# An opening in another order: modulation pieces ahead of the input, six tiles from slots and banks of their own, and heads, gates and projections rearranged

## The chip, the cores and the metric

The kernel runs on one core of a Trainium2 chip. The metric is the device time of one execution in microseconds (us); of several runs the median is taken. A core has five engines with queues of their own, which work through their instructions in order: TensorE (PE, with PEld for its weight loads), VectorE (DVE), ScalarE (ACT), GpSimd (POOL) and SyncE (SP, which here only issues DMAs). They wait for each other through semaphores. PSUM, the memory that TensorE writes to, has eight banks of 128 partitions by 512 float32.

## What is computed

One layer of a decoder: a Mamba-2 mixer and a mixture of experts, both modulated by a vector c. `x` is 512 tokens by 1024 features, all in float32. The reference, cut to what matters here:

```python
c_act = jax.nn.silu(c)
mod = c_act @ ada_w + ada_b                      # 1024 -> 6 * 1024
sh1, sc1, g1, sh2, sc2, g2 = split(mod, 6)
hin = x * (1.0 + sc1) + sh1
z, xbc, dt = split(hin @ w_in, [2048, 2048 + 3072])        # 32 columns are dt
xbc = silu(causal_depthwise_conv(xbc, conv_w, conv_b))     # 4 taps
dt = softplus(dt + dt_bias); a = -exp(a_log)               # 32 heads in 4 groups
y = ssd_chunked_scan(xs, dt, a, bm, cm) + d_skip * xs      # decay, state, y
y = y * silu(z)
y = rms_norm(y, per group of 512) * norm_g
x = layer_norm(ALPHA * x + (1.0 + g1) * (y @ w_out), ln1_g, ln1_b)
hin = x * (1.0 + sc2) + sh2
eid, wts = route(hin, router_w, router_b)                  # 2 of 16 experts
x = layer_norm(ALPHA * x + (1.0 + g2) * moe_ffn(hin, eid, wts, ...), ln2_g, ln2_b)
```

## The kernel before

**Stages.** The program has three: the opening (to 98 us), four turns, one for each of the four head groups of eight heads (98 to 484 us, the fourth of them written out as the last turn), and the experts (from about 500 us to the end). All work is ordered by hand: each engine has its own block of code, and its instructions run in the order in which they stand there. SyncE's block is the order of nearly all loads.

**How a float32 product is made.** A weight unit is 128 by 1024 float32 (512 KB). ScalarE rounds it to the shorter type fp32r (`unit_high`, L712), GpSimd subtracts that from the original (`unit_low`, L566), and TensorE multiplies high by high, high by low and low by high. So one tile of a projection is 8 chunks x 3 = 24 products of 128x512 (L1576 to L1578). Raw units are staged in two slots of `stage`, the split ones in two slots of `wsplit`; s_uh, s_ul and s_unit count highs, lows and finished tiles, and SyncE may load a unit when the low half of the unit two before it is made.

**The opening.** SyncE loads c, the input `x` (four DMAs into `oacc`), then eight pieces of `ada_w` of 128x2048 float32 (1 MB; the last in two halves, 7a and 7b), then weight units. ScalarE's queue issues the small loads (ld_small) and w_dt, the 32 dt columns of w_in (ld_wdt). VectorE sums the pieces, each times a column of silu(c), into `accA` (L1009, L1014); row 0 of accA was first filled with ada_b through a DMA that waits for two memsets (L348), and before its first sum VectorE copies the transposed small rows out of PSUM (L1000 to L1004). TensorE transposes x, and from accA makes shift and scale as columns (modulation products, s_modp), which VectorE copies to `modc`. Then come `hin = x * (1 + scale) + shift` (L1031), its high half by ScalarE (L719), its low half by GpSimd or VectorE (L572, L1020), the products for dt (L1601 to L1603), and six x tiles of group 0: B, C and four of xs.
Each tile goes through `conv0` (ScalarE, last tap with bias, L741, reads the tile's bank), three more taps (VectorE, `xbc_tile`, L1048, read the same bank) and SiLU (ScalarE, L747). Two banks are used in turn, so tile i waits for the taps of tile i-2 (s_cv). Between the taps stand the dt steps on VectorE (L1239 to L1289): softplus of dt (with an exponential and a logarithm by ScalarE and a reciprocal, L1255), dt times a, a running sum (L1267), splitting of that into halves, four scalings by `gmask` into `acg`, a cast of `every8` (L1283), and the weights of the state. From these TensorE makes the products L1610 and transposes L1614 behind tile 5. GpSimd sets `oacc` to zero (L579) once x has been transposed, and sends it by two DMAs to the buffer in DRAM in which the experts' results are added (L582).

**A turn.** For each of the eight heads VectorE scales (`seg_head`, L1058), ScalarE takes exponentials (L755, L758), VectorE mixes (`mix_head`, L1067), GpSimd makes the decayed C (L589), and TensorE makes rows of decays (L1621) and, for two heads at once, y (`y_pair`, L1644 and L1646). Four state steps (`state_step`, L1080 to L1086) stand among the heads. `skip` and `gate` (L1143, L1150) follow for four pieces q of y, then squares (ScalarE) with their sums (GpSimd, L602), high halves of y (ScalarE) and low halves (VectorE, L1193), and TensorE's sums of squares (L1816). ScalarE's `zcopy` (L751) empties the banks of the z tiles. In between TensorE makes the next group's tiles and projects y with w_out.
In the last turn there is no next group. TensorE makes three pieces of the gate vector g1 (`mod_piece`, L1653) instead, two between y_pair(1) and y_pair(2) and one behind y_pair(3), then the sums of squares, and then the projection with w_out (`project`, L1676 to L1678), which waits for all four low halves. Thereafter a residual, layer norm and the routing lead to the experts.

## Time and profile before

| | |
|---|---|
| Runs of the kernel | 1084.26 us median of 3 (1082.76 to 1088.03) |
| Profiled execution | 1094.05 us, its span 1092.3 us |
| Granted TensorE clock, mean of the span | 0.979 of full speed |
| Busy share of the span | TensorE 94%, VectorE 83%, ScalarE 57%, GpSimd 42% |
| DMA | 285.17 MB, mean 261 GB/s |

The profile is of one execution. The span runs from the first instruction to the last. What each row says: in the timeline, a start and a length in us, the engine, the line of the kernel, the operation, what it writes and reads, and in brackets how long its engine had been idle, and which engine, buffer and line ended that. A clock of 1.00 in a stretch is the higher of TensorE's two levels (2.4 GHz), 0.50 the lower (1.2 GHz). Names of engines with a q behind (SPq) are the queue's own instructions, which issue DMAs.

### The profile page before, as it was taken

The numbers are of one execution on the slowest core, as the hardware profiler recorded it, in microseconds if no ns is written. First come the engines' busy times: TensorE is split into PE (matmuls) and PEld (weight loads), VectorE is DVE, ScalarE is ACT, GpSimd is POOL, SyncE is SP. The second block draws the span as 40 slices with busy tenths as digits, with TensorE's granted clock in tenths as the row PEclk, the third lists the DMA queues.
The fourth block names the chain that finished last, engine by engine and source line by source line (L and its number), as shares of the span: only waits on it lengthen the run. The fifth ranks groups of instructions, "written<-read, shape, count | busy, mean of one in ns | idle before, by whom it ended". The sixth has DMA issues, their size and how long they took to land.

```text
span 1092.3 us, 14992 instructions
## 1 busy us (share of the span) xinstructions
PE 1032.1 (94%) x4950; PEld 820.1 (75%) x4950; DVE 906.5 (83%) x964; ACT 617.2 (57%) x598; POOL 463.0 (42%) x298
## 2 busy tenths in 40 slices
PE   2697999999999997998999999999999999999997
PEld 2475788778778875874488888888888888888883
DVE  4897878787877877686498999998999999998986
ACT  0363463365256336350377777776777777776761
POOL 1343554465365445107043433244233433244467
PEclk9598999999999999999999999999999999999999
DMA  9337227324622735669389999999999999999992
GB/s 360 91 86 261 59 78 242 95 67 154 191 58 77 239 115 190 267 227 352 138 311 373 383 378 357 392 377 374 358 369 391 378 365 361 382 377 376 372 347 78
DMA packets 100565, 285.17 MB, mean 261 GB/s; under 512 B 9924, under 2 KB 51052, under 8 KB 83255
## 3 DMA queue, kind: packets, MB, share of 16 engines
q1 hardware_dynamic: 93890, 272.73, 68.5%
q0 software_dynamic: 5264, 11.86, 2.8%
q10 hardware_dynamic: 1382, 0.21, 0.1%
q8 instruction: 16, 0.26, 0.1%
q14 instruction: 13, 0.11, 0.0%
HBM read 276.60 MB, written 15.73 MB: 268 GB/s over the span
## 4 chain that ended last, share of the span: by engine, by line
PE 81%; DVE 10%; issue 3%; DMA 2%; ACT 2%; POOL 1%; ACTq 0%; DVEq 0%; SPq 0%; POOLq 0%
PE ps L1886 15%; PE ps L1888 15%; PE ps L1890 15%; PE ps L1576 5%; PE ps L1577 5%; PE ps L1578 5%; PE ps L1907 2%; PE ps L1836 2%; PE ps L1838 2%; PE ps L1837 2%; DVE ssd L1009 2%; PE ps L1879 1%; DMA both<-in_ssd_a_log 1%; PE ps L1870 1%; DVE ssd L1048 1%
## 5 line engine op out<-in xcount | busy, mean ns | idle before, releaser
L1312 DVE TENSOR_TENSOR moe_r<-moe,moe_r 128x2048 fp32r<-128x2048 f32 x180 | 412.7, 2311 | 58.2 <-ACT moe_r L891 58.2
L891 ACT ACTIVATE moe_r<-moe 128x2048 fp32r<-128x2048 f32 x180 | 344.8, 1928 | 124.1 <-PE ps L1890 119.1
L1886 PE MATMUL ps<-moe_r 128*128 128x512 f32 x720 | 211.2, 397 | 0.1
L1888 PE MATMUL ps<-moe_r 128*128 128x512 f32 x720 | 205.8, 390 | 0.0
L1890 PE MATMUL ps<-moe_r 128*128 128x512 f32 x720 | 205.5, 390 | 0.0
L566 POOL TENSOR_TENSOR ssd_r<-ssd,ssd_r 128x1024 fp32r<-128x1024 f32 x56 | 137.0, 2447 | 151.1 <-ACT ssd_r L712 147.2
L1890 PEld LDWEIGHTS ps<-moe_r 128*128 128x128 f32 x720 | 135.2, 188 | 29.1
L1888 PEld LDWEIGHTS ps<-moe_r 128*128 128x128 f32 x720 | 135.1, 188 | 29.1
L1886 PEld LDWEIGHTS ps<-moe_r 128*128 128x128 f32 x720 | 131.9, 188 | 26.6 <-DVE moe_r L1312 0.8
L1576 PE MATMUL ps<-ssd_r 128*128 128x512 f32 x320 | 128.6, 402 | 4.0 <-DVE ssd L1048 4.0
L640 POOL DMA_INDIRECT ydram<-moe,moe_i x14 | 31.1, 2225 | 224.7 <-DVE moe L1430 224.7
L1577 PE MATMUL ps<-ssd_r 128*128 128x512 f32 x320 | 125.8, 393 | 0.0
L1578 PE MATMUL ps<-ssd_r 128*128 128x512 f32 x320 | 125.6, 393 | 0.0
L630 POOL TENSOR_SCALAR moe_r<-both,moe_r 128x128 fp32r<-128x128 f32 x68 | 102.0, 1512 | 3.6 <-POOL moe_r L626 3.6
L712 ACT ACTIVATE ssd_r<-ssd 128x1024 fp32r<-128x1024 f32 x54 | 56.9, 1053 | 42.1 <-PE ps L1838 36.8
L1576 PEld LDWEIGHTS ps<-ssd_r 128*128 128x128 f32 x320 | 60.7, 190 | 19.4 <-DVE ssd L1048 4.4
L1577 PEld LDWEIGHTS ps<-ssd_r 128*128 128x128 f32 x320 | 60.8, 190 | 13.1 <-issue 1.0
L1578 PEld LDWEIGHTS ps<-ssd_r 128*128 128x128 f32 x320 | 60.8, 190 | 13.0
L1048 DVE SCALAR_TENSOR_TENSOR ssd<-ps,ssd 128x511 f32<-128x511 f32 (+2 forms) x72 | 56.6, 786 | 10.1 <-ACT ssd L741 8.3
L626 POOL CAST moe_r<-moe 128x20 fp32r (+1 forms) x17 | 16.5, 971 | 93.3 <-PE ps L1860 93.3
L589 POOL TENSOR_TENSOR ssd<-ssd 128x384 f32<-128x384 f32 x32 | 37.4, 1178 | 41.5 <-ACT ssd L758 41.5
L1058 DVE TENSOR_SCALAR ssd<-ps,ssd 128x128 f32<-128x128 f32 x128 | 43.7, 404 | 10.1 <-PE ps L1621 7.5
(302 smaller groups left out, 1474.7 us busy)
## 6 DMA issues: line engine op xcount, KB each, us to landing
moe<-in_moe_w_up SPq DMA_DIRECT2D x116, 1024.0 KB, 7.1
moe<-in_moe_w_down SPq DMA_DIRECT2D x64, 1024.0 KB, 8.0
ssd<-in_ssd_w_in SPq DMA_DIRECT2D x40, 512.0 KB, 4.0
ssd<-in_ada_w SPq DMA_DIRECT2D x30, 512.0 KB, 4.7
raw<-in_moe_w_up SPq DMA_DIRECT2D x12, 1024.0 KB, 7.7
ssd<-in_ssd_w_out SPq DMA_DIRECT2D x16, 512.0 KB, 4.7
ssd<-in_ada_w SPq DMA_DIRECT2D x4, 1024.0 KB, 16.4
ydram<-both POOLq DMA_DIRECT2D x2, 2048.0 KB, 13.0
```

The costliest lines, as they stand in the source:

```text
L566: pool.tensor_tensor(to[:, 1, :], stage[:, slot, :], to[:, 0, :].bitcast(F32), ALU.subtract).then_inc(s_ul, 1)
L630: op = pool.tensor_scalar(sel[:, t, :], iota, tabc[:, t, 4:5].bitcast(F32), None, ALU.is_equal)
L712: act.activation(wsplit[:, slot, 0, :], stage[:, slot, :], ACT.Identity).then_inc(s_uh, 1)
L891: act.activation(wr[:, part_slot(i), 0, :], ring[i % RING], ACT.Identity).then_inc(s_wh, 1)
L1048: op = dve.scalar_tensor_tensor(conv[:, i % 2, s:], ps[:, i % 2, 0:T - s], gtaps[:, k, i:i + 1], conv[:, i % 2, s:], ALU.mult, ALU.add)
L1312: dve.tensor_tensor(wr[:, part_slot(i), 1, :], ring[i % RING], wr[:, part_slot(i), 0, :].bitcast(F32), ALU.subtract).then_inc(s_wl, 1)
L1576: mm(to, wh[:, k, :], hin[:, 0, k, :], start=(k == 0), stop=False)
L1577: mm(to, wh[:, k, :], hin[:, 1, k, :], start=False, stop=False)
L1578: op = mm(to, wl[:, k, :], hin[:, 0, k, :], start=False, stop=(k == DC - 1))
L1886: mm(to[i], xh, wh[i], start=start, stop=False)
L1888: mm(to[i], xh, wl[i], start=False, stop=False)
L1890: op = mm(to[i], xl, wh[i], start=False, stop=stop)
```

## The change

There are five edits.

1. **SyncE's queue and the sums.** The input is loaded behind ada_w piece five (counted from zero) and ahead of piece six. The two memsets of accA and the DMA of ada_b into its row 0 are gone; the first sum is a plain product of piece zero and a column of silu(c) (L1041), and ada_b comes as 16 more rows of the small loads, is transposed with them and added when shift and scale are read (L1074). The copies of small rows move behind the sixth sum (piece five), together with the group-0 taps (L1026 to L1028) and the sign of a (L1057), which waits for ScalarE's exponential of a_log (s_prea). The sum and cast for `every8` move to the start.
2. **Six slots and five banks.** The six x units of group 0 get raw slots of their own (two of `stage` and four of `modr`, all loaded without a wait), split into `wsplit` by `open_high` and `open_low`. Tiles 0 to 4 write banks 0, 1, 2, 6 and 7, tile 5 bank 1. Tile 5 alone waits for taps (of tile 1). The small products L1610 and L1614 move ahead of it.
3. **ScalarE and GpSimd in the opening.** The reciprocal becomes an exponential of minus the logarithm on ScalarE. ScalarE also makes the high half of the running sum, the four scalings, and issues the two DMAs of zeros. GpSimd's fill of `oacc` moves ahead of the low halves of units two to five.
4. **Heads.** In a turn, the mix of head h-1 stands ahead of the state step of head h.
5. **The last turn.** One gate piece in place of two stands between the y pairs, and two behind them; ScalarE makes high halves 0 and 1 before the third square, and high half 2 before the fourth; the first projection waits for the low halves one by one, and the sums of squares stand behind it.

VectorE ahead of and among the eight sums. The names: ssd holds accA and pieces, `early` the other pieces, s_rowp the transposed small rows, ld_adaA0 to 7 the landing of a piece. Before:

```order
L996 MEMSET ssd_r 128x2048
L1000 COPY both<-ps 128x120 [waits s_rowp,ld_b0,s_cact]
L1001 COPY both<-ps 128x32
L1002 COPY both<-ps 128x16
L1004 COPY both<-both 32x4 [waits s_const]
L1009 SCALAR_TENSOR_TENSOR ssd<-ssd,both 128x2048 [waits ld_adaA0]
L1009 SCALAR_TENSOR_TENSOR ssd<-early,both,ssd 128x2048 [waits s_adaA,ld_adaA1]
...
L1009 SCALAR_TENSOR_TENSOR ssd<-early,both,ssd 128x2048 [waits s_adaA,ld_adaA5]
L1009 SCALAR_TENSOR_TENSOR ssd<-ssd,both 128x2048 [waits s_adaA,ld_adaA6]
L1014 SCALAR_TENSOR_TENSOR ssd<-early,both,ssd 128x2x512 [waits ld_adaA7,s_adaA]
L1014 SCALAR_TENSOR_TENSOR ssd<-early,both,ssd 128x2x512 [waits ld_ada1]
```

After:

```order
L1041 TENSOR_SCALAR ssd<-ssd,both 128x2048 [waits ld_adaA0,s_cact]
L1044 SCALAR_TENSOR_TENSOR ssd<-early,both,ssd 128x2048 [waits s_adaA,ld_adaA1]
...
L1044 SCALAR_TENSOR_TENSOR ssd<-early,both,ssd 128x2048 [waits s_adaA,ld_adaA5]
L1049 COPY both<-ps 128x120 [waits s_rowp]
...
L1053 TENSOR_SCALAR both<-ps 128x4x2
L1026 COPY ssd<-both 128x5 [waits s_rowc]
...
L1057 TENSOR_SCALAR both<-both 32x1 [waits s_prea,s_gtap]
L1044 SCALAR_TENSOR_TENSOR ssd<-ssd,both 128x2048 [waits s_adaA,ld_adaA6]
L1062 SCALAR_TENSOR_TENSOR ssd<-early,both,ssd 128x2x512 [waits ld_adaA7,s_adaA]
L1062 SCALAR_TENSOR_TENSOR ssd<-early,both,ssd 128x2x512 [waits ld_ada1]
```

The five copies and the taps now stand between pieces five and six, and with them a wait for s_prea, on which every later sum hangs.

GpSimd from the low half of unit zero to the turns, first before:

```order
L566 TENSOR_TENSOR ssd_r<-ssd,ssd_r 128x1024 [waits s_uh]
L572 TENSOR_TENSOR ssd_r<-ssd,ssd_r 128x512 [waits s_hinh]
L566 TENSOR_TENSOR ssd_r<-ssd,ssd_r 128x1024 [waits s_uh] x5
L579 MEMSET both 128x4096 [waits s_xtp]
L582 DMA ydram<-both 128x4x1024 [waits s_const]
L582 DMA ydram<-both 128x4x1024
```

After:

```order
L574 TENSOR_TENSOR ssd_r<-ssd,ssd_r 128x1024 [waits s_uh]
L580 TENSOR_TENSOR ssd_r<-ssd,ssd_r 128x512 [waits s_hinh]
L574 TENSOR_TENSOR ssd_r<-ssd,ssd_r 128x1024 [waits s_uh]
L585 MEMSET both 128x4096 [waits s_xtp]
L574 TENSOR_TENSOR ssd_r<-both,ssd_r 128x1024 [waits s_uh] x4
```

The fill stood behind the low half of unit five; now it stands behind that of unit one, and the DMAs have left this queue.

ScalarE where the dt steps and the first tiles begin; L742 (L729 before) is the logarithm, L851 the new exponential, L754 (L741) conv0, L724 (L712) a rounding. Before:

```order
L729 ACT_TABLE_LOAD
L729 ACTIVATE ssd<-ssd 32x512 [waits s_pre]
L741 ACTIVATE ssd<-ps,ssd 128x512 [waits s_gtap,s_unit]
L712 ACTIVATE ssd_r<-ssd 128x1024 [waits s_unit,ld_u0]
L741 ACTIVATE ssd<-ps,ssd 128x512 [waits s_unit]
L712 ACTIVATE ssd_r<-ssd 128x1024 [waits s_unit,ld_u1]
L747 ACT_TABLE_LOAD
L747 ACTIVATE ssd<-ssd 128x512 [waits s_cv] x2
L741 ACTIVATE ssd<-ps,ssd 128x512 [waits s_silu,s_unit]
L712 ACTIVATE ssd_r<-ssd 128x1024 [waits s_unit,ld_u0]
```

After:

```order
L742 ACT_TABLE_LOAD
L742 ACTIVATE ssd<-ssd 32x512 [waits s_pre]
L851 ACT_TABLE_LOAD [waits s_pre]
L851 ACTIVATE ssd<-ssd 32x512 [waits s_prea]
L754 ACTIVATE ssd<-ps,ssd 128x512 [waits s_gtap,s_unit]
L724 ACTIVATE ssd_r<-both 128x1024 [waits s_unit,ld_y0]
L754 ACTIVATE ssd<-ps,ssd 128x512 [waits s_unit]
L724 ACTIVATE ssd_r<-both 128x1024 [waits s_unit,ld_y1]
L857 DMA ydram<-both 128x4x1024 [waits s_const]
L857 DMA ydram<-both 128x4x1024
L859 ACTIVATE ssd_r<-ssd 32x512 [waits s_pre]
L861 ACTIVATE ssd<-ssd 32x512 [waits s_pre]
```

A table load and an exponential now stand ahead of conv0 of tile 0 and of the rounding of unit two.

TensorE in the last turn; L1653 (L1693 after) are gate pieces, L1644 (L1684) begins a y pair, L1816 (L1769) the sums of squares, L1676 (L1718) the projection. Before:

```order
L1653 MATMUL ps<-ssd,both 128x512 [waits ld_adaA0,s_e]
L1653 MATMUL ps<-ssd,both 128x512 [waits ld_adaA1]
L1644 MATMUL ps<-ssd 64x128 [waits s_y1,s_ch,s_m]
...
L1644 MATMUL ps<-ssd 64x128 [waits s_y1,s_ch,s_m]
...
L1653 MATMUL ps<-ssd,both 128x512 [waits ld_adaA2]
L1816 MATMUL ps<-both,ssd 128x1 [waits s_sqs,s_cbm]
L1676 MATMUL ps<-ssd_r 128x512 [waits s_ul,s_zc,s_yl]
L1676 MATMUL ps<-ssd_r 128x512
L1676 MATMUL ps<-ssd_r 128x512 [waits s_ul]
```

After:

```order
L1693 MATMUL ps<-ssd,both 128x512 [waits ld_adaA0,s_e]
L1684 MATMUL ps<-ssd 64x128 [waits s_y1,s_ch,s_m]
...
L1684 MATMUL ps<-ssd 64x128 [waits s_y1,s_ch,s_m]
...
L1693 MATMUL ps<-ssd,both 128x512 [waits ld_adaA1]
L1693 MATMUL ps<-ssd,both 128x512 [waits ld_adaA2]
L1718 MATMUL ps<-ssd_r 128x512 [waits s_yl,s_ul,s_zc]
L1718 MATMUL ps<-ssd_r 128x512 [waits s_yl]
L1718 MATMUL ps<-ssd_r 128x512 [waits s_yl,s_ul]
L1718 MATMUL ps<-ssd_r 128x512 [waits s_yl]
L1769 MATMUL ps<-both,ssd 128x1 [waits s_sqs,s_cbm]
```

One gate piece moved behind the y pairs, and the sums of squares behind the first twelve products of the projection, which wait for s_yl in four places.

The diff, cut to its core:

```diff
+        x_stage = [stage[:, 0, :], stage[:, 1, :]] + [modr[:, i, :] for i in range(4)]
...
+        x_tile_bank = lambda g, i: (0, 1, 2, 6, 7, 1)[i] if isinstance(g, int) and g == 0 else i % 2
...
-            for t in range(TT):
-                sp.dma_start(oacc[:, t, :], x[0, t * P:(t + 1) * P, :]).then_inc(ld_x, 16)
             for k in range(DC):
+                if k == DC - 2:
+                    for t in range(TT):
+                        sp.dma_start(oacc[:, t, :], x[0, t * P:(t + 1) * P, :]).then_inc(ld_x, 16)
...
-                if k == 0:
-                    sp.wait_ge(s_acc0, 2)
-                    sp.dma_start(accA[0:1, :], ada_b[0:1, 0:2 * D]).then_inc(ld_b0, 16)
...
+                sp.dma_start(x_stage[i].rearrange("p (k n) -> p k n", k=DC), w_v[:, :, x_col(0, i):x_col(0, i) + P]).then_inc(x_ld[i], 16)
...
+            def open_low(i):
+
+                pool.wait_ge(s_uh, i + 1)
+                pool.tensor_tensor(wsplit[:, i % 2, 1, :], x_stage[i], wsplit[:, i % 2, 0, :].bitcast(F32), ALU.subtract).then_inc(s_ul, 1)
...
-                    unit_low(0, 0)
-            unit_low(1, 1)
-            for i in range(2, XU):
-                unit_low(i, i % 2)
+                    open_low(0)
+            open_low(1)
             pool.wait_ge(s_xtp, DC)
             pool.memset(oacc, 0.0).then_inc(s_const, 1)
-            pool.wait_ge(s_const, CONSTS + 1)
-            for a in range(2):
-                pool.dma_start(ydram.rearrange("(a t p) n -> p a t n", a=2, p=P)[:, a], oacc).then_inc(ld_zero, 16)
+            for i in range(2, XU):
+                open_low(i)
...
+            def open_high(i):
+
+                act.wait_ge(x_ld[i], 16)
+                if i >= 2:
+                    act.wait_ge(s_unit, i - 1)
+                act.activation(wsplit[:, i % 2, 0, :], x_stage[i], ACT.Identity).then_inc(s_uh, 1)
...
+                if last:
+                    y_high(g, 0)
+                    y_high(g, 1)
                 square(g, 2)
+                if last:
+                    y_high(g, 2)
                 square(g, 3)
...
+            act.wait_ge(s_prea, 4)
+            act.wait_ge(s_pre, 3)
+            act.activation(dtv[2][0:32], dtv[4][0:32], ACT.Exp, scale=-1.0).then_inc(s_prea, 1)
             for i in range(2):
                 conv0(0, i)
-                unit_high(i + 2, i % 2, 2)
+                open_high(i + 2)
...
+            act.wait_ge(s_const, CONSTS + 1)
+            for a in range(2):
+                act.dma_start(ydram.rearrange("(a t p) n -> p a t n", a=2, p=P)[:, a], oacc).then_inc(ld_zero, 16)
+            act.wait_ge(s_pre, 8)
+            act.activation(ysplit[0:32, 0, 1, :], stk[0:32], ACT.Identity).then_inc(s_prea, 1)
+            act.wait_ge(s_pre, 9)
+            act.activation(dtv[1][0:32], dtv[1][0:32], ACT.Exp).then_inc(s_prea, 1)
             silu(0, 0)
             silu(0, 1)
             conv0(0, 2)
-            unit_high(4, 0, 3)
-            act.wait_ge(s_pre, 10)
-            act.activation(dtv[1][0:32], dtv[1][0:32], ACT.Exp).then_inc(s_prea, 1)
+            open_high(4)
+            act.wait_ge(s_dtv, 4)
+            for g in range(G):
+                act.activation(acg[0:64, g, :], ysplit[0:64, 0, 1, :].bitcast(F32), ACT.Identity, scale=gmask[0:64, g:g + 1]).then_inc(s_prea, 1)
...
-            dve.memset(accA, 0.0).then_inc(s_acc0, 1)
-            dve.wait_ge(s_acc0, 1)
-            dve.memset(accA[32:33, D:2 * D], 1.0).then_inc(s_acc0, 1)
...
+                if k == 0:
+                    dve.tensor_scalar(accA, adaA[0], cact[:, 0:1], None, ALU.mult).then_inc(s_adaA, 1)
+                else:
                     dve.wait_ge(s_adaA, k)
-                dve.scalar_tensor_tensor(accA, adaA[k], cact[:, k:k + 1], accA, ALU.mult, ALU.add).then_inc(s_adaA, 1)
+                    dve.scalar_tensor_tensor(accA, adaA[k], cact[:, k:k + 1], accA, ALU.mult, ALU.add).then_inc(s_adaA, 1)
+                if k == DC - 3:
+                    pairs4 = lambda a: a.rearrange("p (q r) -> p q r", q=4)
+                    own = modb.rearrange("p (q a r) -> p a q r", q=4, a=2)
+                    dve.wait_ge(s_rowp, 3)
+                    dve.tensor_copy(taps, ps[:, 0, 0:120].rearrange("p (k j) -> p k j", k=5)).then_inc(s_rowc, 1)
+                    dve.tensor_copy(normg32, ps[:, 0, 128:160]).then_inc(s_rowc, 1)
+                    dve.tensor_copy(dskip, ps[:, 0, 192:208]).then_inc(s_rowc, 1)
+                    dve.tensor_copy(own[:, 0], pairs4(ps[:, 0, 160:168])).then_inc(s_rowc, 1)
+                    dve.tensor_scalar(own[:, 1], pairs4(ps[:, 0, 168:176]), 1.0, None, ALU.add).then_inc(s_rowc, 1)
+                    dve.wait_ge(s_rowc, 9)
+                    xbc_taps(0)
+                    dve.wait_ge(s_prea, 1)
+                    dve.tensor_scalar(aneg[0:32, :], aneg[0:32, :], -1.0, None, ALU.mult).then_inc(s_dtv, 1)
...
                     seg_head(g, h)
+                    if h:
+                        mix_head(g, h - 1)
                     if h < 3:
                         state_step(g, h)
-                    if h:
-                        mix_head(g, h - 1)
...
-            dve.wait_ge(s_prea, 4)
-            step(dve.reciprocal(uv, uv))
             xbc_tile(0, 0)
+            dve.wait_ge(s_prea, 5)
...
-                if i >= 2:
+                if isinstance(g, int) and g == 0:
+                    if i == NT - 1:
+                        pe.wait_ge(s_cv, 2)
+                elif i >= 2:
                     pe.wait_ge(s_cv, NT * g + i - 1)
-                elif not isinstance(g, int):
+                else:
                     pe.wait_ge(s_zc, ZT * (g - 1) + i + 3)
-                tile(unit_x(g, i), i % 2, bank(i % 2))
+                tile(unit_x(g, i), i % 2, bank(x_tile_bank(g, i)))
...
+                        if i == 0:
+                            pe.wait_ge(s_yl, 4 * (G - 1) + 2 + k)
...
                 y_pair(g, 3)
                 if last:
+                    mod_piece(1)
                     mod_piece(2)
                 if not last:
                     xbc_tile(g + 1, 2)
                     xbc_tile(g + 1, 3)
-                pe.wait_ge(s_cbm, g + 1)
-                pe.wait_ge(s_sqs, 3 * g + 3)
-                for t in range(TT):
-                    op = mm(ps[:, 4, t:t + 1], squares[0][:, t * P:(t + 1) * P], ones[:, 0:1], start=True, stop=True)
-                op.then_inc(s_ms, 1)
-                if not last:
+                if last:
+                    last_tiles()
+                else:
```

## Rows read from the trace of the kernel before

**Rows 1.** The page's part 4: the chain that ended last, by engine:
```profile
PE 81%; DVE 10%; issue 3%; DMA 2%; ACT 2%; POOL 1%; ACTq 0%; DVEq 0%; SPq 0%; POOLq 0%
```

**Rows 2.** Two stretches: length, busy time (instructions) of each engine, clock, DMA:
```profile
292.30:388.10 95.80, 94.98 (x505) 76.55 (x504) 75.51 (x111) 44.25 (x62) 48.54 (x26) 1.00 0.43 131
600.00:700.00 100.00, 100.00 (x471) 83.18 (x470) 91.53 (x62) 74.11 (x53) 40.51 (x27) 1.00 0.98 377
```

**Rows 3.** The chain in order of time, opening: start, length, what:
```profile
18.70 2.36 DVE ssd L1009
...
36.10 1.30 DVE ssd L1014
```

**Rows 4.** ScalarE in the opening: start, length, what [idle before <- releaser]:
```profile
32.31 0.42 ACT L714 ACTIVATE ssd_r<-ssd 128x256 fp32r<-128x256 f32 x1 [26.07 <-DMA ssd<-in_ssd_w_in]
...
34.04 0.20 ACT L716 ACTIVATE both<-both 32x1 f32<-32x1 f32 x1
```

**Rows 5.** Load of piece six: its issue, and KB and us to landing:
```profile
7.79 0.44 SPq L342 DMA_DIRECT2D ssd<-in_ada_w  x1
...
ssd<-in_ada_w SPq DMA_DIRECT2D x1, 1024.0 KB, 22.9
```

**Rows 6.** Hardware queues, 22:24 (both) and 4:6 (SyncE's): packets, MB, share:
```profile
q1 hardware_dynamic: 114, 0.82, 100.0%
q10 hardware_dynamic: 115, 0.01, 5.0%
...
q1 hardware_dynamic: 202, 0.71, 99.9%
```

**Rows 7.** GpSimd, VectorE and ScalarE where the dt steps begin, in order of time:
```profile
51.56 2.40 POOL L566 TENSOR_TENSOR ssd_r<-ssd,ssd_r 128x1024 fp32r<-128x1024 f32 x1 [1.46 <-ACT ssd_r L712]
...
54.26 0.67 DVE L1249 SCALAR_TENSOR_TENSOR ssd<-ssd 32x512 f32<-32x512 f32 x1
...
57.63 3.34 DVE L1255 RECIPROCAL ssd<-ssd 32x512 f32<-32x512 f32 x1 [0.35 <-ACT ssd L729]
...
58.87 0.78 ACT L741 ACTIVATE ssd<-ps,ssd 128x512 f32<-128x512 f32 x1 [1.33 <-PE ps L1578]
```

**Rows 8.** GpSimd and VectorE around the fill of oacc:
```profile
79.34 3.53 POOL L579 MEMSET both<- 128x4096 f32 x1
...
77.00 5.89 DVE L1283 CAST ssd_r<-both 128x8 fp32r<-128x8 f32 x1
```

**Rows 9.** TensorE after two idle times, and the clock after each (stretches):
```profile
84.54 0.80 PE L1576 MATMUL ps<-ssd_r 128*128 128x512 f32 x1 [3.95 <-DVE ssd L1048]
...
86.00:90.00 4.00, 4.00 (x11) 3.13 (x10) 3.90 (x4) 0.00 (x0) 1.38 (x1) 0.50 1.01 409
...
102.62 1.10 PE L1630 MATMUL ps<-ssd 128*128 128x512 f32 x2 [2.43 <-DVE ssd L1165]
...
102.00:103.00 1.00, 0.38 (x1) 0.30 (x2) 1.00 (x3) 0.48 (x1) 0.93 (x1) 1.00 0.00 0
```

**Rows 10.** ScalarE, the sixth SiLU of the opening:
```profile
97.38 0.63 ACT L747 ACTIVATE ssd<-ssd 128x512 f32<-128x512 f32 x1 [2.91 <-DVE ssd L1048]
```

**Rows 11.** VectorE, ScalarE and TensorE in a steady turn, in order of time:
```profile
309.94 2.37 DVE L1067 TENSOR_TENSOR ssd<-ssd 128x512 f32<-128x512 f32 x1
...
314.83 0.59 ACT L751 ACTIVATE ssd<-ps 128x512 f32<-128x512 f32 x1
...
314.99 0.49 PE L1621 MATMUL ps<-ssd_r 128*128 x1 [0.51 <-ACT ssd L758]
...
317.43 0.50 PE L1621 MATMUL ps<-ssd_r 128*128 x1 [0.22 <-ACT ssd L758]
```

**Rows 12.** VectorE and TensorE in the last turn, in order of time:
```profile
430.35 1.72 DVE L1150 TENSOR_TENSOR ssd<-ssd 128x512 f32<-128x512 f32 x1
...
434.22 1.02 PE L1816 MATMUL ps<-both,ssd 128*128 128x1 f32 x8 [2.84 <-POOL ssd L602]
436.67 0.80 PE L1676 MATMUL ps<-ssd_r 128*128 128x512 f32 x1 [1.42 <-DVE ssd_r L1193]
```

129 lines of the change are left out of this document (64 added, 65 removed).

## The prediction

> **What bounds the kernel now.** I read the chain that ended last first, by engine [rows 1]: TensorE carries 81% of the span, so an edit counts only where it removes time in which TensorE waits or runs at its lower clock. Then the stretches [rows 2]: in one whole head-group turn TensorE is busy 94.98 of 95.80 us, and in the expert stage 100.00 of 100, its DMA share 0.98. Nothing in the change touches these stretches except one order of VectorE steps, and every start there hangs on an earlier end, so what is won or lost ahead of them passes to the end one to one. That leaves the opening (0 to 98 us) and the last turn (420 to 445 us).
>
> In the opening the chain is read in order of time [rows 3]: seven weighted sums on VectorE from 18.70 to 36.10, 2.45 us each and 0.2 more for the last, and then the eighth in two halves; the first half, done at 37.39, starts the modulation products. The dense products follow; 24 of them make a projection tile and take 5.44 us (0.227 each at the granted clock 1.00). The tiles run from 53.2 to 80.4 without a gap, and then TensorE waits 3.95 us for a bank that VectorE must free [rows 9]. The opening ends with the sixth SiLU, at 97.38 + 0.63 = 98.01 [rows 10].
>
> **Part 1: the sums.** They now begin with piece one, at the head of the queue, and no longer wait for the small loads: the 18.70 at which they began goes. But between pieces five and six (counting from zero) VectorE now waits for s_prea, the exponential of a_log. ScalarE issues that behind the rounding of the dt weights, and it waits for these until 32.3; rounding, a table load and the exponential end at 34.24 [rows 4], 1.93 later. The sums behind that wait are pieces six (2.45) and 7a (1.25). With the same landing, 7a would end at 34.24 + 0.2 + 3.7 = 38.1, which is 0.7 later than before. Does the landing move? From 22 to 24 us both hardware queues move the same number of packets (114 and 115), and so from 8 us on [rows 6]. SyncE's are then rows of 8 KB and the dt weights are 1024 packets of 128 bytes, which is why they take so long. From 4 to 6 us, when SyncE's packets are the 4 KB rows of the input, it moves 202 in the same time. After the change the input (512 such packets) comes behind piece five, at about 22.6, while some 350 of the 1398 packets of the other queue are left; at up to 200 in 2 us they need some 4 us, and the slowest engines trailed by 3 to 4 before. I take 29.9 as the landing (bounds 28 and 33). Then 7a ends at 29.9 + 1.93 + 0.2 + 3.7 = 35.7, **1.7 us earlier** than 37.39. The gain is bounded by the loads: piece six landed at 7.79 + 22.9 = 30.7 [rows 5] and has the same bytes ahead of it, so 30.7 + 3.7 = 34.4 and 3.0 at most; a landing at 33 would make it a loss of 1.4.
> The input now lands just ahead of piece six, near 28 (1 MB takes 2.6 us at the 0.82 MB in 2 us of [rows 6]). Its transposes end some 6 us later, under cover of the sums until 35.7; should the input come over 2 us later, the rest is lost time.
>
> **Part 2: the dt steps and the six tiles.** I count on the old clock, as if the tiles began at 53.2 again. What goes from VectorE's chain is the reciprocal (3.34 [rows 7]), four scalings, a copy and the 5.89 us row [rows 8]. That last one is a cast of 128x8; it lasted from 77.00 to 82.89, as long as GpSimd was busy, the last 3.53 us of it with the fill of oacc (until 82.87). The fill is not removed. It now stands right behind the rounding of unit one, which ends at 51.56 + 2.40 = 53.96, so it holds GpSimd until 57.5, and that is where the dt steps begin (54.26). A one-input step inside SBUF (L1251) is of the kind that the cast was. It is ready at 55.5 and goes at 57.5. Then: logarithm ready at 58.6 (table already loaded), a new table load 1.28, the exponential that replaces the reciprocal 0.63, so 60.5. On ScalarE conv0 of tile 0 (0.7; at 58.87 before [rows 7]) and the rounding of unit two (1.0) are queued behind it; now they end at 62.2, GpSimd's half (2.38) at 64.65, and tile 2 starts 0.6 late.
> VectorE: taps of tile 0 until 63.55 (2.28); three steps on pairs of SBUF tensors, of which the first waits for that GpSimd half until 64.65 and the next GpSimd half (2.4) slips in behind the third at 66.7; it holds the next step, until 69.1. Scale, copy, scan and difference (0.44, 0.42, 1.40, 0.69) end at 72.05, the low half at 72.8, taps of tile 1 at 75.1. Only then can ScalarE do SiLU 1 (0.6), conv0 of tile 2 (0.7) and, behind them, the rounding of unit four (1.0), and GpSimd its half (2.4): 79.9. Tile 3 has ended at 75.6. So the stall of 3.95 us that own banks remove is followed by one of **4.3 us ahead of tile 4**, for weights. Before, such a stall brought the granted clock to 0.50 [rows 9] and the tile took 8.43 in place of 5.44; I charge the same 2.9. Tile 4 ends at 88.2, the small products 1.4, tile 5 at 95.0, and conv0, taps and SiLU 5 (3.9) end at 98.9: 0.9 later than 98.01. With the 1.7 of part 1 the opening **gains 0.8 us**. The four scalings and two DMA issues that ScalarE takes over lie in its waits, except that the scalings stand ahead of conv0 of tile 3, which has slack.
> Bounds for the steps that no row shows: the two-input first dt step (L1249) may be held by the fill as well (3.3 more at the start, 2.2 at the end, since half of it falls on waits) or not at all, which I take, as the only row of a step held by a fill has one input. The clock may stay up: 2.9 less.
>
> **Part 3: heads reordered.** In a steady turn TensorE idles twice for ScalarE, 0.51 and 0.22 us [rows 11]. The mix of head 1 stood behind a state step and took 2.37 because a rounding on GpSimd ran over it. Moved ahead, head 3's exponentials come 2.4 us earlier and the first wait goes. But the second hangs on zcopy, which can't start before the z tile that TensorE ends at 314.5, 0.2 for the signal, and started at 314.83; the chain behind it is unchanged. So 0.12 us a turn, not 0.7. In the first turn zcopy was late by 0.75. Sum 0.75 + 3 x 0.12 = **1.1 us** (bounds 0 and 3). State steps wait for TensorE with slack, so the other side costs nothing.
>
> **Part 4: the last turn.** TensorE ends the third gate piece at 431.3, waits 2.84 for the sum of squares and 1.42 for the low halves, and runs the first projection from 436.67 to 441.76 at 0.43 a product, half clock [rows 12]. Now gate piece one stands behind y_pair(3). y_pair(2) must wait until 425.75 for GpSimd's last decayed C, so both pairs come 0.4 earlier only, not 1.8. The gates of tiles 2 and 3 collide with GpSimd's square sums as gate 3 did before (1.72 [rows 12] for a step that takes 0.7), so gate 3 ends at 432.06, as before. Gain comes from ScalarE: the high halves are ready, the low halves (0.62 each) start at 432.06, the third or none is held by the last square sum, and they end at 434.6 to 435.9. TensorE works until 432.7 and starts the projection then, at full clock, piece by piece; it ends at 435.5 to 436.6, the square sums 0.6 later, at 437.0 against 441.76: 4.8. VectorE then starts its residuals 3.2 earlier, but TensorE was never held by them for the first six. I take **4.7 us** (bounds 2.5 and 5.5).
>
> **Sum.** 0.8 + 1.1 + 4.7 = 6.6 us. The profiled execution would end at 1094.05 - 6.6 = 1087.5; it is 9.8 above the median of the three runs, and the gain is a sum of waits, so I take it off that median: 1084.26 - 6.6 = **1077.7**. About 0.5% (5.4 us) is what a measurement can tell here.
>
> On the lock, *SBUF — State Buffer* of the Trainium skill (section "SBUF: two separate sides") says that a VectorE step with two SBUF inputs is held only by a GpSimd step that reads SBUF, one in the two-port mode by any; a fill reads nothing, so by it L1249 passes and L1251 is held, as I took it. If the two-input step is held too, that is the first rival. No run here shows a two-input step against a fill.
>
> **Rivals.** (1) The fill holds the two-input step too: everything to tile 4 is 2.2 later, 1079.9. For it: two-input steps are held by roundings [rows 11]. (2) The stall ahead of tile 4 costs no clock, or GpSimd's half doesn't slip in between VectorE's steps: 2.9 us less, 1074.8. For it: an idle time of 2.43 us left the clock at 1.00 [rows 9]; against it: 3.95 did not. (3) The dt weights land no earlier than before, 32.3: part 1 turns from +1.7 to -0.7, 1080.1. (4) Slower: the same wait, with a later landing. It costs one for one; the gain of 6.6 is gone at a landing of 36.5 us, and 0.5% is lost from 42. For it: more weight tiles are queued on SyncE (six in place of two). Against it: they come behind, as packets of 512 bytes that let the other queue pass. (5) The change doesn't do what it says: banks are freed, but the fill holds nothing, as if it were read as a GpSimd step alone: tile 4 without a gap, some 5.5 us more, 1072.
>
> **Chances.** Forecast 0.38, (1) 0.17, (2) 0.15, (3) 0.12, (4) 0.10, (5) 0.08. The range reaches from (5) with 2 more from parts 3 and 4, 1070, to (3) with nothing from part 3 and 2.5 from part 4, 1080.1 + 1.1 + 2.2, and 0.7 for a landing at 33: 1084. Faster by over 0.5% (below 1078.8): most of the forecast (0.28), (2) and (5), 0.51; within 0.5%: the rest of it, (1), (3) and a little of (4), 0.41; slower: 0.08 of (4).
>
> **What would show it.** Part 1: VectorE idle ahead of piece six, released by ScalarE, until about 32. Part 2: the fill near 52, a 2 us step at L1296, a gap ahead of tile 4 of some 4 us with the clock at 0.50 behind it, and none ahead of tile 5. Part 3: turns of 95.7 us. Part 4: no gap over 1.5 us between the gate pieces and the first projection, clock 1.00. It would be wrong if dense products begin later than 51.5 or tile 4 follows tile 3 at once.

## The result, and the profile after

| Group of runs | kernel before, median | of its executions at 1089 or more | changed kernel, median | ratio (95% interval) |
|---|---|---|---|---|
| first | 1091.83 us | 16 of 22 | 1083.85 us (1079.37 to 1087.84) | 0.9944 (0.9926 to 0.9962) |
| c0_after | 1089.74 | 16 of 27 | 1085.25 | 0.9958 (0.9937 to 0.9978) |
| c2_after | 1084.68 | 2 of 35 | 1083.31 | 0.9992 (0.9969 to 1.0014) |

The changed kernel is 0.6% faster in the first group, and its medians in the three lie within 2 us. What moves is the kernel before: its executions lie around two levels, each some us wide, and how many lie at which differs from group to group, which ran on different chips (in three more groups 2 of 29, 3 of 29 and 9 of 17 were at 1089 or more). The mark of 1089 is not sharp: the changed kernel had single executions at 1090.01 and 1091.02. The forecast of 1077.7 us was 6 us too low: 6.6 us were taken off 1084.26, the median of three runs, and that is the lower of the two levels, while the trace they were read from (1094.05) is of the upper. That the ratio of the first group, 0.9944, looks like the forecast (6.6 us are 0.6%) is luck: it depends on how many executions of the kernel before lay on the upper level.

One of the twelve executions of p4_old_opening, a kernel of a later section, took 1754.37 us at a granted clock of 0.559, and its median is given without it.

The profiled execution of the changed kernel took 1085.04 us (span 1083.3, clock 0.986). The chain by engine, from its page; VectorE's share was 10% [rows 1] and is 6%:

```profile
PE 85%; DVE 6%; DMA 3%; issue 2%; ACT 2%; POOL 1%; ACTq 0%; DVEq 0%; POOLq 0%
```

The opening after: ScalarE's rounding of the dt weights, VectorE's sign step with the wait for s_prea, and sum six (start, length, engine, what, idle before and its releaser).

```profile
29.44 0.42 ACT L727 ACTIVATE ssd_r<-ssd 128x256 fp32r<-128x256 f32 x1 [22.28 <-DMA ssd<-in_ssd_w_in]
...
31.47 0.14 DVE L1057 TENSOR_SCALAR both<-both 32x1 f32<-32x1 f32 x1 [7.55 <-ACT both L729]
31.58 2.35 DVE L1044 SCALAR_TENSOR_TENSOR ssd<-ssd,both 128x2048 f32<-128x2048 f32 x1
```

The dt weights landed at 29.44 (32.31 before [rows 4]) and the wait for s_prea is there: 7.55 us, ending at 31.47. The modulation products start at 35.40 (37.53 before).

GpSimd's fill and rounding beside the VectorE steps that they hold, then TensorE at tile 4, its clock behind that, and the sixth SiLU:

```profile
51.76 3.53 POOL L585 MEMSET both<- 128x4096 f32 x1
59.86 2.00 POOL L574 TENSOR_TENSOR ssd_r<-both,ssd_r 128x1024 fp32r<-128x1024 f32 x1 [4.57 <-ACT ssd_r L724]
63.65 2.04 POOL L574 TENSOR_TENSOR ssd_r<-both,ssd_r 128x1024 fp32r<-128x1024 f32 x1 [1.79 <-ACT ssd_r L724]
...
53.13 2.43 DVE L1296 TENSOR_SCALAR ssd<-ssd 32x512 f32<-32x512 f32 x1 [0.77 <-ACT ssd L740]
...
63.87 2.11 DVE L1306 TENSOR_SCALAR ssd<-ssd,both 32x512 f32<-32x512 f32 x1
...
76.04 0.50 PE L1611 MATMUL ps<-ssd_r 128*128 128x512 f32 x1 [2.90 <-POOL ssd_r L574]
...
76.00:80.00 4.00, 3.96 (x12) 3.17 (x13) 2.24 (x3) 2.49 (x4) 1.95 (x1) 0.70 0.51 137
80.00:84.00 4.00, 4.00 (x21) 3.33 (x19) 0.00 (x0) 0.55 (x1) 0.05 (x1) 0.87 0.61 167
...
93.33 0.63 ACT L760 ACTIVATE ssd<-ssd 128x512 f32<-128x512 f32 x1 [1.87 <-DVE ssd L1091]
```

The fill stands at 51.76 and holds a one-input step for 2.43 us (0.41 in e2_fill_late, where the fill stands elsewhere), and the rounding at 63.65 holds another for 2.11 (0.47 there). TensorE waits 2.90 ahead of tile 4 and then runs at 0.50 in part (0.70 over 76 to 80). The SiLU ends at 93.96 against 98.01 [rows 10].

The turns and the last turn: TensorE's waits, and VectorE and GpSimd where the residual begins (L1173 and L1174 are its steps, L1730 TensorE's first transposes of it).

```profile
311.50 0.50 PE L1661 MATMUL ps<-ssd_r 128*128 x1 [0.68 <-ACT ssd L771]
...
426.28 0.47 PE L1718 MATMUL ps<-ssd_r 128*128 128x512 f32 x1 [1.39 <-DVE ssd_r L1198]
...
428.64 0.47 PE L1718 MATMUL ps<-ssd_r 128*128 128x512 f32 x1 [0.73 <-DVE ssd_r L1198]
...
438.42 0.66 PE L1730 MATMUL ps<-both,moe 128*128 128x128 f32 x4 [1.32 <-DVE moe L1174]
...
433.46 2.12 DVE L1173 TENSOR_TENSOR both<-both 128x512 f32<-128x512 f32 x1
435.61 2.76 DVE L1174 SCALAR_TENSOR_TENSOR moe<-moe,both 128x512 f32<-128x512 f32 x1
...
432.58 5.23 POOL L569 TENSOR_TENSOR ssd_r<-ssd,ssd_r 128x1024 fp32r<-128x1024 f32 x2 [4.64 <-ACT ssd_r L837]
```

One wait of 0.68 for ScalarE is left of the two of [rows 11]. In the last turn the waits of 2.84 and 1.42 [rows 12] are now 1.39 and 0.73, and a new one of 1.32 follows at 438.42: the first two residual steps take 2.12 and 2.76 us where later ones take 0.69, while GpSimd rounds units at the same time.

**Where the 9 us between the two traces lie.** I compared the start of the same TensorE instruction in both. The changed kernel is ahead by 4.0 us at the first state product of turn one, 5.0 at the end of that turn, 5.6 and 6.2 after the next two, 6.5 at its last wait for ScalarE in the fourth; by 11.0 at the end of the first projection tile; by 9.65 behind the new wait; by 7.7 when the experts begin, since behind a wait of 2.63 us in the routing the clock stayed at 0.50 for 6.8 us (in the trace of before, behind 2.43 us, for 3.4). Over the experts it gains 1.3 more: each block takes 34.93 us and not 35.03, with the same instructions.

That last part is no chance of one execution. From the same product behind the routing to the same one at the end, the experts take 553.4 to 553.5 us in all thirteen traces with the changed opening, and 554.4 to 554.8 in all seven with the old one, p4_old_opening among them, on whatever chip. So it comes with the changed opening, in whose edits nothing touches the experts' order. Whether it comes through what those edits do or only through the program being another one, no run tells: p6_cast_last, with one useless step more, has 35.00. Each product is some 0.6 ns quicker, evenly over the stage.

### The profile page after: what moved, and what is told of

Same layout as the page of the kernel before. It is cut to its first block, busy times and chain, and to the rows that moved or that the text cites. A ratio compares the mean times of both kernels' runs of the same rounds, so it can differ in the third digit from the quotient of the medians.

```text
span 1083.3 us, 14990 instructions
## 1 busy us (share of the span) xinstructions
PE 1028.6 (95%) x4950; PEld 818.3 (76%) x4950; DVE 895.9 (83%) x958; ACT 619.2 (57%) x603; POOL 462.6 (43%) x296
## 4 chain that ended last, share of the span: by engine, by line
PE 85%; DVE 6%; DMA 3%; issue 2%; ACT 2%; POOL 1%; ACTq 0%; DVEq 0%; POOLq 0%
PE ps L1933 15%; PE ps L1935 15%; PE ps L1937 15%; PE ps L1611 6%; PE ps L1612 6%; PE ps L1613 6%; DMA ssd<-in_ssd_w_in 2%; PE ps L1954 2%; PE ps L1883 2%; PE ps L1885 2%; PE ps L1884 2%; PE ps L1926 1%; PE ps L1917 1%; PE ps L1670 1%; PE ps L1684 1%
## 5 line engine op out<-in xcount | busy, mean ns | idle before, releaser
L569 POOL TENSOR_TENSOR ssd_r<-ssd,ssd_r 128x1024 fp32r<-128x1024 f32 x50 | 123.6, 2473 | 145.1 <-ACT ssd_r L717 140.4
L717 ACT ACTIVATE ssd_r<-ssd 128x1024 fp32r<-128x1024 f32 x48 | 50.6, 1053 | 41.4 <-PE ps L1885 36.3
L1091 DVE SCALAR_TENSOR_TENSOR ssd<-ps,ssd 128x511 f32<-128x511 f32 (+2 forms) x72 | 53.7, 746 | 23.3 <-ACT ssd L754 21.5
```

What stands on the lines that cost most here:

```text
L569: pool.tensor_tensor(to[:, 1, :], stage[:, slot, :], to[:, 0, :].bitcast(F32), ALU.subtract).then_inc(s_ul, 1)
L717: act.activation(wsplit[:, slot, 0, :], stage[:, slot, :], ACT.Identity).then_inc(s_uh, 1)
L1091: op = dve.scalar_tensor_tensor(conv[:, i % 2, s:], ps[:, x_tile_bank(g, i), 0:T - s], gtaps[:, k, i:i + 1], conv[:, i % 2, s:], ALU.mult, ...
```

## Experiments: the kernel before has two branches

**c1_before** is the kernel before, traced again.

> The kernel before, unchanged, for a second trace of it. Its executions so far spread from 1081 to 1095 us, and over 27 of them the span falls as the granted clock of the span rises (0.976: 1092.8; 0.985: 1081.1). Theory: the spread is half clock in stretches of 3.4 or 6.8 us behind waits of TensorE, which come in one execution and not in another, so this trace shows the same waits as the first (3.95 ahead of tile 5, 2.84 and 1.42 in the last turn, 2.43 in the routing) with fewer or shorter stretches at 0.50, if its time is lower, and a difference in time equal to half of the difference in busy half-clock time. Rival: the spread is the pace of loads, and one of the waits is longer by as much.

Its executions had a median of 1085.20 us (1081.26 to 1092.66). The trace is of one with a span of 1084.2, and it has no wait ahead of tile 5. First VectorE and GpSimd in it, then the GpSimd row of the first trace that belongs to [rows 8].

```profile
76.85 0.17 DVE L1283 CAST ssd_r<-both 128x8 fp32r<-128x8 f32 x1
...
79.27 0.68 DVE L1286 TENSOR_TENSOR ssd<-ssd 32x512 f32<-32x512 f32 x1
...
76.86 2.42 POOL L566 TENSOR_TENSOR ssd_r<-ssd,ssd_r 128x1024 fp32r<-128x1024 f32 x1 [3.05 <-ACT ssd_r L712]
79.21 3.53 POOL L579 MEMSET both<- 128x4096 f32 x1
```

```profile
76.99 2.42 POOL L566 TENSOR_TENSOR ssd_r<-ssd,ssd_r 128x1024 fp32r<-128x1024 f32 x1 [3.03 <-ACT ssd_r L712]
```

In the first trace the cast was issued at 77.00, 10 ns after GpSimd's rounding, and took 5.89 us: it got in only when rounding and fill were over. Here it was issued at 76.85, 10 ns before the rounding, and took 0.17. Everything behind differs by that: tile 5 starts at 80.29 without a wait, not at 84.54, and its 24 products take 5.44 and not 8.43. I call these the long branch (cast held, wait ahead of tile 5) and the short branch. Both of my expectations fell in part: the waits are not the same ones, and the one that differs is not longer by the pace of loads. Of the 8.1 us between the two spans 4.8 are in two waits (3.95 ahead of tile 5, and 1.42 against 0.60 in the last turn), and TensorE was busy at half clock for 27.3 us in one and 20.0 in the other, of which half, 3.7, is lost time by my estimate. *SBUF — State Buffer* of the Trainium skill (section "SBUF: two separate sides") describes the port that VectorE and GpSimd share as "an exclusive lock, not a bandwidth split", held for the whole instruction by whichever starts first. By that rule the order of the two starts decides, and these two traces agree. The order that a trace gives is not finer than that, though: in p5_cast_later (below) both starts read 76.86 and the cast took 5.88, in p1_last_alone both read 77.46 and it took 0.17.

**p2_cast_early** takes the cast away from there (kernel before, cast and its sum at VectorE's start):

```diff
+            dve.wait_ge(s_const, CONSTS)
+            dve.tensor_reduce(every8, ident.rearrange("p (a j) -> p j a", j=HG), AX.X, ALU.add).then_inc(s_acc0, 1)
+            dve.wait_ge(s_acc0, 3)
+            dve.tensor_copy(every8r, every8).then_inc(s_acc0, 1)
             dve.wait_ge(s_cact, 1)
...
-            dve.tensor_reduce(every8, ident.rearrange("p (a j) -> p j a", j=HG), AX.X, ALU.add).then_inc(s_dtv, 1)
-            dve.wait_ge(s_dtv, 5 + G)
-            dve.tensor_copy(every8r, every8).then_inc(s_dtv, 1)
...
-            pe.wait_ge(s_dtv, 6 + G)
+            pe.wait_ge(s_dtv, 4 + G)
+            pe.wait_ge(s_acc0, 4)
```

> The kernel before with one thing moved: the sum and the cast that make the eighths (every8) stand at VectorE's start, where it waits for loads anyway. Theory: the two traces of the kernel before differ by 7 us at one place. In one the cast was issued at 77.00 us, 10 ns after GpSimd's low half (76.99), and took 5.89; in the other at 76.85, 10 ns ahead of it (76.86), and took 0.17, and TensorE had no wait ahead of tile 5. So the kernel before has two branches, about 1083 and 1091 us, decided by which of two steps is first. Without the cast there only the short branch is left: no wait ahead of tile 5, median 1082 to 1084, no execution above 1089, 0.994 to 0.999 of the kernel before depending on how many of its executions take the long branch here. Rival: another one-input step (the scalings) then meets the low half, or the spread comes from the clock in other places: it spreads from 1081 to 1094 like the kernel before.

Median 1084.61 us, all twelve executions between 1082.5 and 1087.21, no wait ahead of tile 5. Beside it the kernel before had 1084.68, mostly short, with single ones up to 1092.63: ratio 1.0003 (0.9986 to 1.0019). In p2_cast_early what is left goes in part with the clock: five executions with a granted clock of 0.984 or more have a mean span of 1082.1, seven below that 1084.2.

**p5_cast_later** and **p6_cast_last** push it the other way, with work that serves nothing:

```diff
+            for _k in range(2):
+                dve.memset(sums2[:, _k, :], 0.0)
             dve.wait_ge(s_dtv, 5 + G)
             dve.tensor_copy(every8r, every8).then_inc(s_dtv, 1)
```

and in p6_cast_last

```diff
+            dve.tensor_reduce(sums2[:, 0, 0:HG], ident.rearrange("p (a j) -> p j a", j=HG), AX.X, ALU.add)
             dve.wait_ge(s_dtv, 5 + G)
```

> The kernel before with two fills of 128x16 (some 0.1 us each) on VectorE right ahead of the cast; they serve nothing. Theory: the cast is issued after GpSimd's low half in nearly all executions, so the long branch is taken: it takes 5.5 to 5.9 us, TensorE waits 3.9 to 4.1 ahead of tile 5, and the kernel takes 1089 to 1092, 5 to 7 us more than the other kernel of this group, for 0.2 us of added work. Rival: the two branches come from something else, and the time is that of the kernel before.

> The kernel before with a second sum of 128x128 to 128x8 (0.38 us by its first one) on VectorE right ahead of the cast; it serves nothing. The two small fills moved the cast by only 0.01 to 0.1 us (it was issued in the same 10 ns as GpSimd's step) and the long branch came in 4 of 10 executions, against 2 of 35 of the kernel before beside it. With 0.38 us the cast is always behind. Theory: all executions take the long branch, 1089 to 1095 us, median 1091, that is 1.005 to 1.007 of the kernel before where that has a median of 1085; the cast takes 5.5, TensorE waits 4 us ahead of tile 5. Rival: with more room VectorE does something else than wait for the whole fill (the fill begins 2 us later), and executions at 1083 remain.

```profile
76.86 5.88 DVE L1285 CAST ssd_r<-both 128x8 fp32r<-128x8 f32 x1
...
76.86 2.40 POOL L566 TENSOR_TENSOR ssd_r<-ssd,ssd_r 128x1024 fp32r<-128x1024 f32 x1 [3.03 <-ACT ssd_r L712]
```

```profile
76.89 5.69 DVE L1284 CAST ssd_r<-both 128x8 fp32r<-128x8 f32 x1
...
76.70 2.40 POOL L566 TENSOR_TENSOR ssd_r<-ssd,ssd_r 128x1024 fp32r<-128x1024 f32 x1 [3.03 <-ACT ssd_r L712]
...
84.23 0.50 PE L1577 MATMUL ps<-ssd_r 128*128 128x512 f32 x1 [3.94 <-DVE ssd L1048]
```

The two fills (first fence) cost 0.08 us and not 0.2, so the cast came within 10 ns of the rounding: four of ten executions were at 1089.78 to 1095.66, six at 1082.12 to 1085.97, so my "nearly all" was wrong, median 1085.13. With the second sum of 0.37 us (second fence) the cast is issued 0.19 behind the rounding, and by the times it is always late: twelve of twelve at 1088.91 to 1095.41, median 1092.63, while the kernel before beside it had 1089.66 with 9 of 17 at 1089 or more. So one useless step of 0.37 us puts the kernel 8 us over p2_cast_early (on another chip), and 7 over the executions under 1089 of the kernel before beside it. The two levels are this one race. Why the cast comes late more often in one group than in another stays open.

**c0_after** and **c2_after**, the changed kernel again (table above):

> The changed kernel itself, unchanged, as the level for the others of this group on the same chip. Expected: 0.9944 of the kernel before (interval 0.9926 to 0.9962), and a trace with the opening's places as before to 0.1 us: tile 4 at 76.04, sixth SiLU until 93.96. If the time of the turns or of the experts differs from the first trace by some tenths of a per cent with the same instructions, that is the spread of executions and not of the change.

> The changed kernel again, beside the others of this group. On three chips the kernel before had medians of 1090 to 1092 twice and 1085 twice; the changed one 1083.9 and 1085.3. Theory: the changed one has no long branch, so it stays at 1083 to 1085 here too, whatever the kernel before does: a ratio near 0.999 where the latter's median is 1085, near 0.994 where it is 1090. Rival: both move together with the chip, and the ratio stays at 0.994 to 0.996.

The sixth SiLU of c0_after came 0.6 us earlier than in the first trace although the sums ended 1.0 later: behind the same wait of 2.90 us its clock stayed at 1.00. Between the tiles and the first turn it has one half-clock stretch of 3.4 us, at 99.2, and the first trace has two, at 77.6 and 94.7. So my expectation of the same places to 0.1 us was wrong by up to 1 us.

**p4_old_opening** is the kernel before with the cast at the start, the reordered heads and the new last turn, so all of the change but its opening.

> The kernel before with the cast at VectorE's start, the heads reordered and the edit of the last turn, so all of the change but the opening (input behind piece five, sums from piece zero at 7 us, six slots and banks, the exponential for the reciprocal, the fill ahead). Theory: against the short branch of the kernel before the changed opening loses: its sixth SiLU began at 93.56 and 94.19 us, that of the short branch at 91.0, in spite of sums that end 2 us earlier. So this kernel is 2.5 us faster than the changed one (0.998 of it), some 1080 to 1082. Rival: the opening of the change is worth its 1.7 us or more once the clock's chances are evened out, and this one is as slow as the changed kernel or slower.

Median 1080.40 us, ratio 0.9956 (0.9939 to 0.9973), and the changed kernel beside it 1083.31. So the changed opening costs 2.9 us against the short branch, what it brings in the experts included, and heads and last turn bring 4.2 (from 1084.61). From the first modulation product to the start of the sixth SiLU the traces show 52.2 to 53.8 us where the cast was early (c1_before, p1_last_alone, p2_cast_early, p4_old_opening) and 59.4 to 59.85 where it was late. The changed kernel shows 57.9 in its first trace and 56.3 in c0_after and c2_after.

## Experiments: the parts of the changed kernel

**e1_sign_late**: the sign step and its wait behind the sums.

```diff
-                    dve.wait_ge(s_prea, 1)
-                    dve.tensor_scalar(aneg[0:32, :], aneg[0:32, :], -1.0, None, ALU.mult).then_inc(s_dtv, 1)
...
             hin_low(DC - 1)
+            dve.wait_ge(s_prea, 1)
+            dve.tensor_scalar(aneg[0:32, :], aneg[0:32, :], -1.0, None, ALU.mult).then_inc(s_dtv, 1)
```

> The sign step of a with its wait for the exponential of a_log stands behind the eight sums, at the head of the dt steps. Theory: in the changed kernel piece six had landed at 28.9 us and 7a at 30.2, and the wait held the sums until 31.47. Freed, sum six ends at 31.3 and 7a at 32.6 in place of 35.2: the modulation products start at 32.8 instead of 35.40, all of the opening comes 2.6 us earlier and the kernel ends 2.6 earlier (0.24%). Rival: the loads decide, the sums move by under 0.5 us; or the 2.6 us are eaten behind them, because dt products and tile 0 wait for something that doesn't move (weight units, the copies of x), so that tile 0 starts at 51.1 as in the changed kernel.

The modulation products start at 33.63 us (36.36 in c0_after of the same group, 35.40 in the first trace), so the wait costs 1.8 to 2.7 us. The median of six is 1082.26, 3.0 under c0_after.

**e2_fill_late**: the fill and its DMAs back on GpSimd behind unit five.

> GpSimd fills oacc behind the low half of unit five and sends the zeros itself, as in the kernel before; all else as in the changed kernel. Theory: the 2.43 us of the one-input dt step are the fill's, so it takes 0.42 here, the logarithm and the new exponential come 2.0 earlier, and since conv0 of tile 0 waits for tile 0 (to about 57) its chain comes 1.0 to 1.5 earlier; the wait ahead of tile 4 falls from 2.90 to 1.4 to 1.9 us, and with a shorter wait the clock stays at 1.00 behind it (1.7 us at most). The kernel ends 1 to 3 us earlier than the changed one. Rival: the step is held by the low half of unit one, which ends at 51.8, or by something else, and stays at over 2 us; or the fill, now at about 80, holds a VectorE step there and takes back what was won: no change.

```profile
54.24 0.41 DVE L1296 TENSOR_SCALAR ssd<-ssd 32x512 f32<-32x512 f32 x1 [0.77 <-ACT ssd L743]
...
64.65 2.49 DVE L1310 TENSOR_TENSOR_SCAN ssd<-both,ssd 32x128 f32<-32x128 f32 x2
...
64.70 2.16 POOL L574 TENSOR_TENSOR ssd_r<-both,ssd_r 128x1024 fp32r<-128x1024 f32 x1 [2.99 <-ACT ssd_r L727]
...
76.02 0.50 PE L1611 MATMUL ps<-ssd_r 128*128 128x512 f32 x1 [2.28 <-POOL ssd_r L574]
```

The step takes 0.41 us, so the 2.43 were the fill's. Only 1.1 us of it arrive at tile 4 (its start minus that of the modulation products is 39.5 and not 40.6), and the wait is 2.28: the rounding of unit three now holds the scan (the second line of the fence is its held part), 3.12 us in place of 1.36. I had expected a wait of 1.4 to 1.9; the clock stayed at 1.00 behind it, as expected. Median 1082.22 us. The changed kernel did not run in this group: the kernel before had 1085.24, and e6_turned_late, the changed kernel but for one tile's place, 1084.62, so the fill's place is worth some 2.4 us.

**e3_round4_early**: ScalarE rounds unit four ahead of the high half of the running sum.

```diff
+            open_high(4)
             act.wait_ge(s_pre, 8)
...
             conv0(0, 2)
-            open_high(4)
```

> ScalarE rounds unit four ahead of the high half of the running sum, not behind two SiLUs and conv0 of tile 2. Theory: the 2.90 us that TensorE waits ahead of tile 4, and the 3.4 us at half clock behind it, come from ScalarE's order alone: unit four could be rounded when tile 2 ends (67.3) and was rounded at 72.87. Then tile 4 starts at 72.7 to 73.0 with the clock at 1.00 and ends at 78.2 in place of 83.4. Unit five is not moved: its rounding stays behind the scalings, so a new wait of 1 to 2 us stands ahead of tile 5, and the sixth SiLU ends 3 to 4 us earlier than 93.96; the kernel ends 3 to 4 us earlier (0.3%). Rival: the taps of tile 1 and the dt steps are what is late (VectorE is busy from 58.95 to 75.4): the earlier GpSimd half holds them longer, the scalings end later, and what is won ahead of tile 4 is lost ahead of the small products and tile 5: under 1 us in all.

```profile
81.53 0.59 PE L1611 MATMUL ps<-ssd_r 128*128 128x512 f32 x1 [1.69 <-POOL ssd_r L574]
```

No wait is left ahead of tile 4, but 1.69 us ahead of tile 5, with half clock behind. The sixth SiLU starts 56.5 us behind the first modulation product, against 57.9 and, in c0_after, 56.3: next to that trace nothing is won. In the first turn TensorE then waited 3.26 us for a VectorE sum whose weights landed late. Median 1083.01, 2.2 under c0_after; but its trace is 1.0 us behind that of c0_after ahead of the routing and 2.7 ahead behind it, where it has no half clock and c0_after has 6.8 us, so the edit is not shown to have won them. The order of ScalarE's queue causes the wait ahead of tile 4, as I had it; moved alone it passes a shorter one on to tile 5.

**e4_heads_back** undoes the order of heads.

> The mix of head h-1 stands behind the state step again, as in the kernel before; all else as in the changed kernel. By the prediction's working the reordering is worth 0.75 us in the first turn and 0.12 in each other, 1.1 in all. By the comparison of the two traces it is worth 0.9 in the first turn, 0.6 in the second and third and 0.3 in the last, 2.4 in all, half of it at two places (the first wait for ScalarE, and a wait of 0.37 for VectorE ahead of the projection with w_out, which is gone in the changed kernel). So this one ends 1.1 or 2.4 us later than the changed kernel, and the wait of 0.37 is back or not.

Median 1087.80 us, 2.6 above c0_after; at the same TensorE instruction, the first transposes of the residual, its trace is 2.5 us behind, of which 0.8 are sums that ended later: 1.7 for the heads. The waits of 0.51 and 0.22 are back. That of 0.3 to 0.4 for VectorE ahead of the projection is in both kernels in some turns and missing in others, so part of the 2.4 that I had read from two traces was not a fixed gain.

**e5_last_back** (last turn as before), **e5b_highs_back** (only ScalarE's order as before) and **p1_last_alone** (the last turn's edit on the kernel before):

> The last turn as in the kernel before (two gate pieces between the y pairs, ScalarE's high halves behind the fourth square, the sums of squares and one wait for all low halves ahead of the projection); all else as in the changed kernel. By the two traces the edit is worth 4.5 us at the end of the first projection's twelve products, of which 1.4 go again in a new wait for the residual ahead of the first transposes: so this one ends 3.1 us later than the changed kernel, the half clock in the first projection is back (its products 0.43 apart), and the new wait of 1.32 is gone. By the prediction's working it ends 4.7 later. Rival: the gain of this part was the clock alone (3 us), and where the clock doesn't fall in the undone version it is worth under 2.

> The changed kernel with ScalarE's high halves of the last turn behind the fourth square again; TensorE's new order stays. By the prediction the gain of the last turn comes from ScalarE: without it the first low half starts 1.9 us later (three highs at 0.62 each behind the square) and the projection with it, 1.5 to 2.5 us of the 4.5 are lost, and the wait ahead of the projection grows from 1.39 to about 3. Rival: TensorE's order alone (the projection ahead of the sums of squares, so without their wait of 2.84) carries the gain: under 0.7 us lost.

> The kernel before with the edit of the last turn alone (gate piece one behind the y pairs, high halves ahead of the squares, low halves waited for one by one, sums of squares behind the first twelve products). By the two traces this part is worth 3.1 us net (4.5, less 1.4 in the new wait for the residual), by the prediction 4.7. Expected 0.9971 of the kernel before (3.1 us), the products of the first projection 0.23 apart and not 0.43, and the wait of 1.3 ahead of the first transposes of the residual. Rival: the part pays only together with the reordered heads, which bring the last turn's VectorE steps earlier: under 1.5 us.

TensorE where the projection begins, in the three:

```profile
429.32 1.02 PE L1765 MATMUL ps<-both,ssd 128*128 128x1 f32 x8 [2.84 <-POOL ssd L607]
431.76 0.79 PE L1713 MATMUL ps<-ssd_r 128*128 128x512 f32 x1 [1.42 <-DVE ssd_r L1193]
```

```profile
431.07 0.77 PE L1713 MATMUL ps<-ssd_r 128*128 128x512 f32 x1 [3.28 <-DVE ssd_r L1193]
```

```profile
426.34 0.47 PE L1686 MATMUL ps<-ssd_r 128*128 128x512 f32 x1 [1.40 <-DVE ssd_r L1201]
...
438.50 0.66 PE L1698 MATMUL ps<-both,moe 128*128 128x128 f32 x4 [1.32 <-DVE moe L1139]
```

I measured from the second ScalarE wait of that turn (the only one left in the changed kernel) to the first transposes of the residual. It is 32.0 us in every trace with the new last turn and this order of the fourth tile, p1_last_alone among them; it is 35.06 in e5_last_back, 34.4 in e5b_highs_back and 34.15 to 35.16 in the five traces of the kernel before and its variants with the old last turn. So the edit is worth 2.1 to 3.15 there, most of it through ScalarE's order (2.4 of 3.05 on the changed kernel), as the prediction said, and it doesn't need the reordered heads. How much it is goes with the clock: with the old last turn TensorE was busy at half clock for 3.4 to 5.8 us there, with the new one never. By medians: 1087.09 (beside 1084.62 of e6_turned_late), 1087.12 (no changed kernel in its group; the kernel before had 1084.91), and p1_last_alone 1083.36 against 1084.91 of the kernel before, which the interval (0.9971 to 1.0015) does not tell from nothing, nor from 3 us.

**e6_turned_late** moves the fourth projection tile ahead of the first transposes:

> In the last turn TensorE makes the fourth projection tile ahead of the first transposes of the residual and not behind them. Theory: the wait of 1.32 us ahead of these transposes comes from VectorE, whose residual steps GpSimd's low halves hold (2.12 and 2.76 us for steps of 0.69), and 2.8 us of products hide it: no wait there, the routing starts 1.3 us earlier, the kernel ends 1.3 earlier (0.12%). Rival: VectorE is behind for good after the collision, each later tile waits for a residual step, and the 1.3 us come back as waits of 0.3 to 0.5 ahead of the next tiles.

```profile
441.27 0.66 PE L1730 MATMUL ps<-both,moe 128*128 128x128 f32 x4 [1.16 <-DVE moe L1174]
```

The wait comes 2.8 us later, ahead of the second transposes, and is 1.16. From that turn's ScalarE wait to the first wait of the routing this takes 83.9 us and not 84.1, so 0.2 us are won: the rival. VectorE is behind, not TensorE's order wrong.

**b1_all** and **b1_again**: the moves of e1, e3 and e6, unit five rounded ahead of the second SiLU, and the fill between the low halves of units four and five.

```diff
             open_low(1)
+            for i in range(2, XU - 1):
+                open_low(i)
             pool.wait_ge(s_xtp, DC)
             pool.memset(oacc, 0.0).then_inc(s_const, 1)
-            for i in range(2, XU):
-                open_low(i)
+            open_low(XU - 1)
...
-            act.wait_ge(s_const, CONSTS + 1)
-            for a in range(2):
-                act.dma_start(ydram.rearrange("(a t p) n -> p a t n", a=2, p=P)[:, a], oacc).then_inc(ld_zero, 16)
+            open_high(4)
             act.wait_ge(s_pre, 8)
...
             silu(0, 0)
+            open_high(5)
             silu(0, 1)
             conv0(0, 2)
-            open_high(4)
...
             conv0(0, 3)
-            open_high(5)
+            act.wait_ge(s_const, CONSTS + 1)
+            for a in range(2):
+                act.dma_start(ydram.rearrange("(a t p) n -> p a t n", a=2, p=P)[:, a], oacc).then_inc(ld_zero, 16)
```

> Four edits together on the changed kernel: the sign step behind the sums, ScalarE rounds unit four ahead of the high half of the running sum and unit five ahead of the second SiLU, GpSimd fills oacc between the low halves of units four and five (the DMAs of zeros behind conv0 of tile 3), and the fourth projection tile stands ahead of the first residual transposes. Theory: modulation products at 33.6, tiles 0 to 5 without a wait (0.3 at most ahead of tile 5) at full clock, so that the sixth SiLU ends at 87 to 88 in place of 93.96, and 1.3 more in the last turn: 7 to 8 us under the changed kernel, some 1077, 0.988 of the kernel before. Rival: what is won in the opening is lost in the first turn, where VectorE waits for gate weights whose loads don't come earlier (3.26 us in one trace of this group): 3 to 4 us under it only.

> The four edits on the changed kernel together once more (1075.29 us by six executions before). Theory: the level belongs to the kernel, since it has neither the wait ahead of tile 4 nor the cast beside GpSimd's step: 1074 to 1077 here too, 0.991 of the kernel before where that has 1085, and no execution above 1080. Rival: it has two branches of its own that six executions didn't show, and some come to 1080 or more.

1075.29 us (1074.1 to 1076.89) and 1076.06 (1075.12 to 1077.82), on two chips, one of which has the kernel before at 1085.24 and one at 1089.66 (ratios 0.9915 and 0.9877). That is 7 to 10 us under the three medians of the changed kernel, which ran on other chips. The tiles run without a wait, and the sixth SiLU of b1_all ends at 87.84. It beats both kernels.

**w1_keep_clock** adds products of zeros to b1_all, 32 while TensorE waits for the input and 8 while it waits for the sums.

> The kernel with four edits together, and TensorE makes 32 products of zeros into an unused bank while it waits for the input, and 8 while it waits for the last sum. They change no result. In its traces so far the clock falls at 33 us and stays at 0.50 for 13.7 us, over the modulation products and the first dt products, at 6 to 7 us of lost time by the busy share. Theory: the idle time of 7 to 8 us ahead of the transposes of x and of 2.3 to 4.6 behind them is what lowers the clock; without it the modulation products run at 1.00 and the dt products begin 3 to 5 us earlier (VectorE's scalings of x, 0.8 each, are next in line), so 1071 to 1073 in place of 1075.3. Rival: the modulation products themselves (one column each) let it fall, whatever stood ahead; then it falls some us later, and under 1.5 us are gained.

```profile
34.00:37.00 3.00, 2.85 (x27) 2.80 (x27) 2.92 (x7) 1.26 (x2) 0.84 (x1) 1.00 1.15 281
37.00:41.00 4.00, 4.00 (x19) 2.39 (x18) 3.93 (x9) 2.79 (x5) 2.17 (x3) 0.60 0.92 236
41.00:45.00 4.00, 3.01 (x12) 1.04 (x10) 3.89 (x3) 1.28 (x4) 4.00 (x3) 0.97 0.03 7
85.00:89.00 4.00, 3.30 (x16) 2.90 (x16) 3.41 (x7) 3.96 (x5) 0.00 (x0) 0.58 1.03 374
495.00:502.00 7.00, 6.60 (x11) 3.38 (x12) 0.29 (x2) 0.00 (x0) 2.79 (x6) 0.52 0.82 305
```

The half clock of 13.7 us in the opening (from 33.6 in b1_all) shrinks to 3.4, the dt products begin at 38.21 and not at 41.96, and the last turn comes 3.3 us earlier. My forecast of 1071 to 1073 was wrong: the median is 1075.85 all the same (ratio 0.9916, b1_all 0.9915). In this trace 6.8 us of half clock behind a wait of 2.58 in the routing take 3.3 back. Whether that is chance or follows from the work ahead, I did not settle.

## The prediction, step by step

- **What bounds the kernel: right, but for the experts.** What was won or lost ahead of the experts passed to the end, less what the clock took in the routing. "Nothing in the change touches these stretches" did not hold in time: the experts became 1.3 us shorter, by a cause that stays open.
- **Part 1, the sums: right in mechanism, and about in size.** The wait for s_prea, the landing (29.44; I had 29.9) and the start of the modulation products (2.1 us earlier in the first trace; 1.7 forecast). Over all traces the gain is 1.0 us on average (seven of the kernel before or with its opening, nine of the changed one or with its wait).
- **Part 2, the six tiles: right in mechanism, wrong in size.** The fill stood at 51.76, L1296 took 2.43 us, L1306 was held by a rounding, and the wait came ahead of tile 4, where it had been forecast. It was 2.90 us and not 4.3: the three roundings of new slots that stand one behind another up to tile 4 take 2.00 to 2.04 us each and not 2.4, which makes 1.2 of the 1.4. The clock cost 1.9 us (tile 4 took 7.4 and not 5.44) or nothing, not 2.9. Against the long branch the opening gained 4.0 us, not 0.8. The first rival (the fill holds two-input steps) falls: at 79.27 in c1_before such a step took 0.68 beside a fill that had begun at 79.21. (Its price was also off by its own words: half of 3.3 is 1.65, not 2.2.) By the rule of *SBUF — State Buffer* of the Trainium skill that the prediction weighed, the fill should let a two-input step pass, and the trace agrees.
- **Part 3, heads: right, too small.** 1.1 us forecast, 1.7 in the trace of e4_heads_back, within the bounds; by medians it is 2.6, of which the later sums of that trace may be a part. I had counted two waits of TensorE and not the third, of 0.37 ahead of the projection.
- **Part 4, the last turn: right, then incomplete.** 4.7 us forecast, 4.5 at the end of the first projection tile, through ScalarE as said. The sentence that failed is "TensorE was never held by them for the first six": it was, since the residual steps moved into GpSimd's roundings, and 1.4 went again.
- **The sum: here the prediction failed.** It reads "it is 9.8 above the median of the three runs, and the gain is a sum of waits, so I take it off that median". A wait of the profile can only be taken off runs that have it. The largest term of part 2, the 3.95 us ahead of tile 5 and the 2.99 behind it, was in the profiled execution and, by their times, not in the three runs' median. The difference of 9.8 us was the sign of this, and I read past it. Set against the long branch the terms of the two traces are 4.0 + 2.4 + 3.1 = 9.5 us, of which the clock in the routing took 1.9 and to which the experts add 1.3; the medians of the first group differ by 8.0. Against the short branch the opening loses 2.9 and heads and last turn bring 4.2, a gain of 1.3 on one chip (p2_cast_early less c2_after, from which both terms come, so this is no second check), where the forecast had 6.6.
- **The rows that could have told.** [rows 8] shows a cast of 128x8 at 5.89 us. I took its 5.89 us as its price. Beside it stood a GpSimd step that had begun 10 ns earlier (76.99, a row that I did not show), and a start as close as that can fall the other way.

## What to carry to other kernels

When a profiled execution is a per cent above the other runs, find the wait that they may not have before any term of it goes into a sum. Where a VectorE step and a GpSimd step that holds it start within some 10 ns of each other, either may be first, from one execution to the next: the way out is to move the small step to where nothing is beside it (p2_cast_early narrows 1081 to 1093 us to 1082 to 1087), and an edit that does this by the way looks like a gain of 0.6% in one group of runs and of 0.1% in another. A wait for weights that moves from tile to tile has to be followed to the last tile; from the modulation products to the sixth SiLU one moved rounding gave nothing against c0_after (56.5 and 56.3 us), both of them and the fill 2.7 (53.6).

## What the runs showed of the hardware

- A VectorE cast of 128x8 took 0.17 or 5.7 to 5.9 us, depending on whether it was issued 10 ns ahead of a GpSimd rounding or 10 to 190 ns behind it (with both starts at the same reading, each came once); issued behind, it waited through two GpSimd instructions in a row, the rounding and the fill.
- A GpSimd fill held a one-input step inside SBUF and not a two-input one: 2.43 us for L1296 beside the fill (0.41 without), 0.68 for L1286 beside one in c1_before.
- The experts' products ran 0.3% quicker in every trace of a program with the changed opening (34.93 us a block) than in those of the kernel before (35.03), though their instructions are the same; with one added VectorE step in the opening of the latter it was 35.00 (p6_cast_last). No run shows the cause.
- The same wait does not always lower TensorE's clock. Behind 2.90 us ahead of tile 4 it stayed at 0.50 for 3.4 us in one trace of the changed kernel and not at all in two others; behind 1.85 to 2.8 us in the routing for 3.4 or 6.8 us, or not at all (2.57 in c1_before, 2.65 in c2_after). A stretch of 3.4 us in which TensorE is busy for 2.8 to 3.4 costs 1.4 to 1.7 us, an estimate at half of the busy time. Over 27 executions of the kernel before, the span falls from 1092.8 to 1081.1 as its granted clock rises from 0.976 to 0.985; that holds both levels, and the long branch has more half clock itself.
